# A causal long convolution in a two-block network on one NeuronCore: copies of four shifts in one DMA, four more taps on TensorE for the last chunk, and a layer norm through Ln and Exp

## The reference

```
def conformer_conv(x, pw1_w, pw1_b, dw_w, dw_b, ln_g, ln_b, pw2_w, pw2_b):
    h = x @ pw1_w + pw1_b
    a, g = jnp.split(h, 2, axis=-1)
    h = a * jax.nn.sigmoid(g)
    h = causal_dwconv(h, dw_w, dw_b)      # 31 taps, one filter per channel
    h = layer_norm(h, ln_g, ln_b)
    h = jax.nn.silu(h)
    return h @ pw2_w + pw2_b
```

## Time and profile before

| | us |
|---|---|
| median of 3 runs | 1998.79 (1995.87 to 1998.98) |
| the profiled execution, whole | 1995.84 |
| its span, first to last instruction | 1994.1 |
| pw1 stage, TensorE's slot 0 to the end of taps(7) | 640 to 773 |
| first product of the pw2 stage | 784.04 |

### The profile page before, as it was taken

One profiled execution on the slowest core, in us unless ns is written; L12 is line 12 of the kernel. 1 busy time (PEld: TensorE's weight loads), 2 busy tenths in 40 slices (PEclk: granted clock), 3 DMA queues, 4 the chain that ended last, 5 costly groups with the idle time before them and its releaser, 6 DMA issues.

```text
span 1994.1 us, 23337 instructions
## 1 busy us (share of the span) xinstructions
PE 1902.5 (95%) x9196; PEld 1530.5 (77%) x9196; DVE 1063.6 (53%) x1285; ACT 764.3 (38%) x981; POOL 172.5 (9%) x120
## 2 busy tenths in 40 slices
PE   6999999999999996999999999899899999999996
PEld 4767788877788664888888888788777888888885
DVE  6874442255445788745555533643575545555434
ACT  5532332255324445442223222643673632322223
POOL 5500000000002354010000000200000200000001
PEclk9999999999999998999999999999999999999998
DMA  9211222311222444122322333133002123232321
GB/s 391 85 64 64 84 91 99 105 43 43 85 84 85 129 137 130 64 85 85 105 90 99 105 106 106 64 106 105 2 1 96 64 84 104 85 105 86 125 87 61
DMA packets 32588, 186.38 MB, mean 93 GB/s; under 512 B 4865, under 2 KB 7041, under 8 KB 12034
## 3 DMA queue, kind: packets, MB, share of 16 engines
q1 hardware_dynamic: 30928, 175.90, 26.1%
q10 hardware_dynamic: 1586, 9.44, 1.2%
HBM read 174.64 MB, written 2.10 MB: 89 GB/s over the span
## 4 chain that ended last, share of the span: by engine, by line
PE 87%; ACT 5%; DVE 3%; issue 2%; DMA 1%; POOL 1%; SPq 0%; ACTq 0%; DVEq 0%
PE PS L571 24%; PE PS L573 24%; PE PS L572 24%; PE PS L1064 2%; PE PS L961 2%; PE PS L637 1%; PE PS L638 1%; PE PS L639 1%; DMA RAW<-w 1%; PE PS L931 1%; PE PS L912 1%; ACT X L1474 1%; ACT WH L1110 1%; PE PS L1038 1%; PE PS L1075 1%
## 5 line engine op out<-in xcount | busy, mean ns | idle before, releaser
L571 PE MATMUL PS<-H,WH 128*128 128x512 f32 (+1 forms) x1616 | 625.1, 387 | 26.2 <-POOL L L443 13.2
L572 PE MATMUL PS<-L,WH 128*128 128x512 f32 (+1 forms) x1616 | 617.3, 382 | 0.0
L573 PE MATMUL PS<-H,WL 128*128 128x512 f32 (+1 forms) x1616 | 617.2, 382 | 0.0
L1666 DVE TENSOR_TENSOR WL<-RAW,WH 128x2048 fp32r<-128x2048 f32 x136 | 314.8, 2315 | 269.3 <-ACT WH L1110 265.0
L571 PEld LDWEIGHTS PS<-H,WH 128*128 128x128 f32 x1616 | 305.4, 189 | 98.6 <-issue 18.7
L1110 ACT ACTIVATE WH<-RAW 128x2048 fp32r<-128x2048 f32 x144 | 274.8, 1909 | 238.0 <-PE PS L573 183.4
L573 PEld LDWEIGHTS PS<-H,WL 128*128 128x128 f32 x1616 | 305.2, 189 | 59.2
L572 PEld LDWEIGHTS PS<-L,WH 128*128 128x128 f32 x1616 | 305.4, 189 | 57.2 <-issue 0.8
L443 POOL TENSOR_TENSOR L<-X,H 128x512 fp32r<-128x512 f32 x32 | 46.6, 1463 | 1310.0 <-ACT H L1476 750.8
L1545 ACT ACTIVATE TT<-TT 128x512 f32<-128x512 f32 x44 | 27.8, 632 | 310.3 <-DVE TT L2328 310.3
L571 PE MATMUL PS<-FH,WH 128*128 128x512 f32 (+1 forms) x376 | 142.8, 380 | 0.0
(11 more groups left out here) (339 smaller groups left out, 2483.4 us busy)
## 6 DMA issues: line engine op xcount, KB each, us to landing
RAW<-w SPq DMA_DIRECT2D x148, 1024.0 KB, 4.9
HS<-HC SPq DMA_DIRECT2D x128, 65.5 KB, 2.0
ADA<-w_ada ACTq DMA_DIRECT2D x4, 1024.0 KB, 24.2
ADA<-w_ada SPq DMA_DIRECT2D x4, 1024.0 KB, 23.1
GA<-w_gate SPq DMA_DIRECT2D x1, 4096.0 KB, 18.2
PWR<-w_ple ACTq DMA_DIRECT2D x2, 1024.0 KB, 5.1
out<-X SPq DMA_DIRECT2D x8, 256.0 KB, 2.1
X<-x_t SPq DMA_DIRECT2D x2, 512.0 KB, 6.5
```

The source lines that it names most:

```text
L571: nc.tensor.matmul(ps, wh, xh, start=start, stop=False, skip_group_check=skip)
L572: nc.tensor.matmul(ps, wh, xl, start=False, stop=False, skip_group_check=skip)
L573: return nc.tensor.matmul(ps, wl, xh, start=False, stop=stop, skip_group_check=skip)
L1666: v.tensor_tensor(WL[:, p], RAW[:, p], WH[:, p].bitcast(F32), ALU.subtract).then_inc(w_lo, 1)
```

## The change

Six things are changed.

1. `stack(m)` issues four copies in place of 16. Each has 128 rows by 528 columns and reads each of 32 channel rows four times, at shifts 0 to 3. The diagonal weights are laid out to match.
2. SP's loop has `stack(m)` ahead of `load(pw1+2+m)`.
3. The last chunk has 20 taps on TensorE (20 matmuls, 20 diagonal blocks) and 11 on DVE, whose partial sums for it go to another pair of PSUM banks.
4. ACT squares chunk 5 in `pw1(6)`, behind the diagonals of chunk 7; POOL adds chunks 5 and 6 and their squares ahead of the last `weight_lo`, that of slot pw2+1.
5. TensorE adds the last chunk and its square to the means itself, by products with `CV` and `SQV` behind the product with `ACCV`; the four DVE instructions L2139 and L2143 are gone.
6. The deviation of this norm comes from Ln and Exp on ACT; the two reciprocals on DVE are gone. `I32` is made on POOL, before the w_out stage ends, in place of DVE.

```diff
-HSW = T + TAPS * (QUADS - 1)
+HSW = T + TAPS * QUADS
...
-            for m in range(KC):
+            for m in range(KC - 1):
                 weight_lo(SLOT0["pw1"] + m + 2)
                 if m >= 2:
                     chunk_sum(m - 2)
-                if m >= 2:
                     chunk_squares(m - 2)
-            chunk_sum(KC - 2)
-            chunk_squares(KC - 2)
+            for c in (KC - 3, KC - 2):
+                chunk_sum(c)
+                chunk_squares(c)
+            weight_lo(SLOT0["pw1"] + KC + 1)
...
                 for g in range(4):
-                    for k in range(TAPS):
-                        sp.dma_start(HS[32 * k:32 * k + 32, m % 2, g, :],
-                                     HC[32 * g:32 * g + 32, m, k:k + HSW]).then_inc(hs_in[m % 2], 16)
+                    rows_g = HC[32 * g:32 * g + 32, m, 0:HSW]
+                    shifted = bass.AP(rows_g.tensor, rows_g.offset, [list(rows_g.ap[0]), [1, TAPS], [1, HSW]])
+                    sp.dma_start(HS[:, m % 2, g, :], shifted).then_inc(hs_in[m % 2], 16)
...
             for m in range(KC):
+                stack(m)
                 load(SLOT0["pw1"] + 2 + m)
-                stack(m)
...
-                for q in range(QUADS):
+                quads = QUADS + (m == KC - 1)
+                for q in range(quads):
...
-            ln_stats("conv", 0)
-            ln_stats("conv", 1)
+            pe.wait_ge(cv_sum, KC - 2)
+            pe.wait_ge(cv_sq_sum, KC - 2)
+            for h in range(2):
+                nc.tensor.matmul(PS[:, 4 + h, :], MEANC.to_broadcast([P, P]), ACCV[:, h].rearrange("p a t -> p (a t)"),
+                                 start=True, stop=False, skip_group_check=True)
+            for h in range(2):
+                pe.wait_ge(cv_ready, KC + h)
+                nc.tensor.matmul(PS[:, 4 + h, 0:HT], MEANC.to_broadcast([P, P]), CV[:, KC - 1, cols(h)], start=False,
+                                 stop=True, skip_group_check=True)
+                pe.wait_ge(st_acc, 2 * LN_AFTER["conv"] + h + 1)
+                nc.tensor.matmul(PS[:, 4 + h, HT:T], MEANC.to_broadcast([P, P]), SQV[:, (KC - 1) % 2, cols(h)], start=False,
+                                 stop=True, skip_group_check=True).then_inc(lst_ps, 1)
...
-                if stage == "conv":
-                    a(VAR[:, h], VAR[:, h], ACT.Sqrt, bias=EPS_LN).then_inc(lstd_ready, 1)
-                    return
...
-                if stage == "conv":
-                    own.did(v.reciprocal(PS[:, 4 + h, HT:T], VAR[:, h]))
...
-                taps = DW_K - PE_TAPS
+                tap0 = LAST_TAPS if final else PE_TAPS
+                taps = DW_K - tap0
...
-                    if n == 6 and not (isinstance(s.val(), int) and s.val() == 0):
+                    if n == (4 if final else 6) and not (isinstance(s.val(), int) and s.val() == 0):
...
             ln_var("conv", 1)
+            ln_center(1, 0, CV)
             ln_rstd("conv", 0)
```

More of the change, by code:

```diff
@@ L48 @@
 PE_TAPS = TAPS * QUADS
-HSW = T + TAPS * (QUADS - 1)
+LAST_TAPS = PE_TAPS + TAPS
+HSW = T + TAPS * QUADS
 FFN = 2816
@@ L232, in build @@
         CV = at("CV", A + 20, [P, KC, T])
-        DG = at("DG", A + 36, [P, 2, QUADS, P])
+        DG = at("DG", A + 36, [P, 2, QUADS + 1, P])
         HS = at("HS", A + 44, [P, 2, 4, HSW])
@@ L493, in _ @@
                 nc.gpsimd.tensor_tensor(GA[:, m, :], GA[:, m, :], CROWS[:], ALU.mult).then_inc(gate_mul, 1)
+            nc.gpsimd.memset(I32[:], 1.0).then_inc(i32_ready, 1)
+            for n, (base, cm) in enumerate(((0, 1), (TAPS - 1, -1))):
+                pool.wait_ge(i32_ready, n + 1)
+                nc.gpsimd.affine_select(out=I32[:], in_=I32[:], compare_op=ALU.is_ge, fill=0.0, base=base,
+                                        pattern=[[-TAPS * cm, 32]], channel_multiplier=cm).then_inc(i32_ready, 1)
             ln_lo("w_out", L, X, H)
-            for m in range(KC):
+            for m in range(KC - 1):
                 weight_lo(SLOT0["pw1"] + m + 2)
@@ L661, in ln_stats @@
                     return
-                sums = ACCV if stage == "conv" else ACC
-                nc.tensor.matmul(PS[:, 4 + h, :], MEANC.to_broadcast([P, P]), sums[:, h].rearrange("p a t -> p (a t)"),
+                nc.tensor.matmul(PS[:, 4 + h, :], MEANC.to_broadcast([P, P]), ACC[:, h].rearrange("p a t -> p (a t)"),
                                  start=True, stop=True).then_inc(lst_ps, 1)
@@ L952, in taps @@
                 pe.wait_ge(dg_ready, m + 1)
-                pe.wait_ge(hs_in[m % 2], 16 * 4 * TAPS * (m // 2 + 1))
+                pe.wait_ge(hs_in[m % 2], 16 * TAPS * (m // 2 + 1))
                 if m == KC - 1:
@@ L961, in taps @@
                         mm = nc.tensor.matmul(PS[r, 6 + m // (KC - 1), :], DG[:, p, q, r],
-                                              HS[:, p, g, TAPS * q:TAPS * q + T], start=q == 0, stop=q == QUADS - 1,
+                                              HS[:, p, g, TAPS * q:TAPS * q + T], start=q == 0, stop=q == quads - 1,
                                               skip_group_check=True)
@@ L1413, in diagonals @@
                     act.wait_ge(cp_ps, m - 1)
-                for q in range(QUADS):
+                for q in range(QUADS + (m == KC - 1)):
                     for g in range(4):
@@ L1418, in diagonals, with chunk_square, whole_square @@
                 ins.then_inc(dg_ready, 1)
-            def chunk_square(m, cc=slice(0, T)):
-                a(SQV[:, m % 2, cc], CV[:, m, cc], ACT.Square).then_inc(cv_sq, 1)
+            def chunk_square(m):
+                a(SQV[:, m % 2, :], CV[:, m, :], ACT.Square).then_inc(cv_sq, 1)
+            def whole_square(c):
+                if c < 2:
+                    act.wait_ge(cv_moved, c + 1)
+                else:
+                    act.wait_ge(cv_ready, c + 1)
+                    act.wait_ge(cv_sq_sum, max(c - 2, 1))
+                chunk_square(c)
             def pw1(m):
@@ L1428, in pw1 @@
                 split_hi(Step(0), 1, SLOT0["pw1"] + m + 2)
[L1429 to L1436, removed]
+                if 2 <= m < KC - 1:
+                    whole_square(m - 2)
                 if m + 1 < KC:
                     diagonals(m + 1)
-            act.wait_ge(i32_ready, 1)
+                if m == KC - 2:
+                    whole_square(KC - 3)
+            act.wait_ge(i32_ready, 3)
             diagonals(0)
@@ L1443, in _ @@
                 pw1(m)
[L1444 to L1447, removed]
+            tables("natural_log_exp_and_others")
+            whole_square(KC - 2)
             act.wait_ge(cp_ps, KC)
             load_ple(0)
-            act.wait_ge(cv_sq_sum, KC - 4)
+            act.wait_ge(cv_sq_sum, KC - 3)
             for h in range(2):
                 act.wait_ge(cv_ready, KC + h)
-                chunk_square(KC - 1, cols(h))
+                a(SQV[:, (KC - 1) % 2, cols(h)], CV[:, KC - 1, cols(h)], ACT.Square).then_inc(st_acc, 1)
             def ln_std(stage, h):
@@ L2064, in _ @@
             own.did(v.memset(HC[:, :, 0:PAD], 0.0))
-            v.tensor_tensor(I32[:], SEL[:, 0:32].bitcast(F32), SEL[:, 32:64].bitcast(F32), ALU.add).then_inc(i32_ready, 1)
             def pw1(s):
@@ L2077, in pw1 @@
                 hc = rows(HC, s.val(), 1)
-                dsts = (PS[:, 4:5, :], PS[:, 5:6, :])
-                taps = DW_K - PE_TAPS
+                spare = 2 * (1 - p) if final else 4
+                dsts = (PS[:, spare:spare + 1, :], PS[:, spare + 1:spare + 2, :])
+                tap0 = LAST_TAPS if final else PE_TAPS
+                taps = DW_K - tap0
                 cv = rows(CV, s.val(), 1)
                 for n in range(taps):
-                    k = PE_TAPS + n
+                    k = tap0 + n
                     w_ = dcol("dw_w", s.val(1, k * KC))
@@ L2135, in _ @@
                 v.tensor_tensor(last[:, cols(h)], last[:, cols(h)], PS[:, 7, cols(h)], ALU.add).then_inc(cv_ready, 1)
[L2136 to L2144, removed]
             ln_var("conv", 0)
@@ L2155, in _ @@
                 ln_scale(0, p, CV)
-            for p in range(NP):
+            ln_scale(1, 0, CV)
+            for p in range(1, NP):
                 ln_center(1, p, CV)
@@ L2449, in _params @@
         par[:, PCOL[name]:PCOL[name] + c.shape[1]] = c
-    dw = np.asarray(i["a_dw_w_2"]).reshape(DW_K, KC, 4, 32)[0:PE_TAPS].reshape(QUADS, TAPS, KC, 4, 32)
-    par[:, PCOL["dw_s"]:PCOL["dw_s"] + KC * QUADS * 4] = dw.transpose(1, 4, 2, 0, 3).reshape(P, KC * QUADS * 4)
+    dw = np.asarray(i["a_dw_w_2"]).reshape(DW_K, KC, 4, 32)[0:LAST_TAPS].reshape(QUADS + 1, TAPS, KC, 4, 32)
+    par[:, PCOL["dw_s"]:PCOL["dw_s"] + KC * QUADS * 4] = dw[0:QUADS].transpose(4, 1, 2, 0, 3).reshape(P, KC * QUADS * 4)
+    par[:, PCOL["dw_s"] + KC * QUADS * 4:PCOL["dw_b"]] = dw[QUADS, :, KC - 1].transpose(2, 0, 1).reshape(P, 4)
     par[0:SSM_HEADS, PCOL["small_b"]] = i["dt_bias"]
```

2 lines of the change are left out of this document (1 added, 1 removed).

## The result

| | before | after |
|---|---|---|
| median of the runs | 1998.88 us (4 runs) | 2043.47 us (4 runs, 2042.23 to 2048.18) |
| ratio | | 1.023, interval 1.021 to 1.025 |
| span of the profiled execution | 1994.1 us | 2040.8 us |
| mean granted clock | .989 | .978 |

The changed kernel is 44.6 us slower. The forecast was 2016, with a range up to 2026: the sign and the mechanism held, the size did not.

What follows compares the result with a forecast made beforehand. TensorE bounded the pw1 stage but for three places; the change was to be read on ACT's queue. 8L - 51 with L = 8.8 gave +19.4 on 1995.84, so 2015.2; the forecast was 2016 us, range 2003 to 2026.

Steps and rivals of the forecast that it cites:

- The loop: pw1 stage, through ACT's queue: sigmoid, HC, stack, load, rounding, diagonals, next sigmoid; the last sigmoid comes 22.9 us later.
- L: Time from HC written to load landed: 7.5 us at best, 8.8 taken, 9.5 at most.
- 8L - 51: Change of the whole kernel's time in us: +19.4 with L = 8.8, +9.0 with 7.5, +25.0 with 9.5.
- the 0.4: Norm behind the last chunk: with Ln and Exp on ACT the seventh pair comes 0.4 us earlier.
- The tail: Last sigmoid to ACT's squared mean: 9.4 + L = 18.2 us, 3.1 earlier than the 21.3 before.
- the upper end: L of 9.5 us, for a load queued behind copies whose data move at 233 GB/s; the sum is +25.0.
- The head: stack(0) is out after 2.5 us, not 10.11; taps(0) saves some 4 us, which the late second sigmoid swallows.
- in a shadow: Last chunk: taps(7) with 20 taps ends 14.3 us behind the sigmoid at the latest, the last load's path later.
- Rival 2: pw1 stage: the loads stay covered, L below 6.4 us, and the kernel is faster, 1987 us; chance of faster 0.11.
- some 9 earlier: Part of Rival 2: ACT's squared mean comes some 9 us earlier, stack(7) landing 6.3 instead of 12 after HC.
- Rival 1: Stack copies in pw1: their data hide behind the issues, L = 7.5, so +9.0 and 2005 us; chance 0.2.

Runs made afterwards that it cites:

- after_0213: The changed kernel with its four copies issued in the order of groups 0, 2, 1, 3: 2042.70 us, ratio 1.0212.
- sixty_four: The changed kernel with each copy reading 64 rows twice, so the taps get wrong rows: 2038.85 us, ratio 1.0198.
- wide_source: The changed kernel with each copy reading 128 rows once, so the taps get wrong rows: 2011.06 us, ratio 1.0063.
- swap_only: The kernel before with only the order swapped, each load behind its stack of 16 copies: 2076.54 us, ratio 1.0391.
- load_first: The changed kernel with each load ahead of its stack again, the rest of the change kept: 1991.06 us, ratio 0.9963.
- copies_only: The kernel before with four copies in place of sixteen and `I32` made on POOL, loads still ahead of stacks: 1991.62 us, ratio 0.9967.

## Why the prediction was right in kind and wrong in size

**The loop: right.** Eight loads are waited for, the sigmoids don't wait, the squares of steps 2 and 3 wait for POOL inside the loop (5.85 and 5.84 us, 5.98 forecast), TensorE waits for `WL` (six times, for the three forecast), the gap ahead of taps(7) stays (15.1 us), the square of chunk 6 stands behind the last rounding. The sigmoids stand 18 to 21 us apart, and 25 between steps 2, 3 and 4, for the 15 to 17 and 20 to 23 forecast: wider by about the error in L.

**The formula 8L - 51: right.** L is the mean over the eight steps from the end of the write of `HC` to the start of the rounding; the third column puts it into the formula, the last is the difference of the medians.

| kernel | L, us | 8L - 51 | measured |
|---|---|---|---|
| changed kernel | 11.97 | +44.8 | +44.6 |
| after_0213 | 11.82 | +43.6 | +43.2 |
| sixty_four | 11.37 | +40.0 | +39.3 |
| wide_source | 7.89 | +12.1 | +13.0 |
| swap_only | 15.56 | +73.5 | +78.5 |

Four kernels with the same rest of the stage fall within 1 us of it. swap_only doesn't have the shorter tail for which the 51 stands. Inside the traces, from the first sigmoid to ACT's squared mean, the four take 43.7, 42.5, 38.9 and 11.4 us more than the kernel before. That is 7.9 us for each us of L, and 1.1 to 1.5 us less than the sum has there (8L - 50.6, without the 0.4). So the match with the medians to 1 us has some luck in it, and the factor of eight has not. The tail holds by itself in the changed kernel: 9.4 + 12.0 = 21.4, measured 21.3.

**The step that failed: L.** The prediction took 8.8 and gave 9.5 as the upper end, "1.7 + 4.6 + 3.2", with 4.6 us for the data of four copies "at 233 GB/s" from rows 8. In step 0 of the changed kernel the last of the four copies was issued at 657.77 and landed after 5.4 us, at 663.2: 8.1 us behind the first issue, for 1.7 + 4.6 = 6.3 in the sum. The load landed 3.9 us later, for 3.2:

```profile
L561 SPq DMA_DIRECT2D HS<-HC x1: 1699/1699/1699, 657.8 to 657.8; - x1
...
DMA to landing us min/median/max: 5.4/5.4/5.4
```

So of the 2.5 us beyond the upper end, 1.8 are the copies' data, and 0.7 the load behind them. What failed is first the rate. With the 156 GB/s of the window above, the data would take 6.9 us and the sum give 11.8, near the measured 12.0; that this fits so well is partly luck, as a window of 2 us isn't the whole stack. The same window in after_0213 shows more, with L as long:

```profile
657.00:659.00 2.00, 2.00 (x10) 1.66 (x9) 2.00 (x4) 0.00 (x0) 0.00 (x0) 1.00 0.91 208
```

Rows 8 show copies that read 32 rows once each, with an issue every 0.63 us and engines half idle. I scaled this to full occupation and took the end for an upper bound, with the thought that a full queue would only be kinder. A copy of another shape was rated by a row of the old shape; wide_source shows that the shape alone moves the rate from 156 to more than 300 GB/s. The same item took the issues as 0.63 each: they were 0.67, 0.60, 1.23 and 1.70. That adds nothing to L by itself (after_0213: shorter issues, L of 11.8).

Each us of error in L counts eight times, and the range had only 0.7 us above my value. The bound of the one term that is multiplied by eight should have been the widest. With the row's own rate as it stood (107 GB/s, no scaling) the copies' data would have been 10.1 us, L 15.0 and the far end +69: that was the upper bound that the nearest row gave.

**The head and the tail.** In the changed kernel the formula, which counts nothing for the head, holds. In load_first the head is worth 4.1 us, as forecast. The tail from the last sigmoid is as long as before (21.3 both times), as L ate the "3.1 earlier"; for L = 12 the formula says so itself. Ln and Exp gain 0.5 us at the seventh pair, for the 0.4 forecast. The 20 taps were costed in a shadow and stand in the path once the loop is open: 0.6 to 1.7 us.

**The rivals.** Rival 2, that the loads stay covered, gave 1987; load_first, where they are, is 1991. Of the "some 9 earlier" that it had at ACT's squared mean the head's 4.1 came, but only 2.0 in the tail, as taps(7) starts 8.1 us behind the write of `HC` and not 6.3, and takes 6.91. Rival 1, that the copies' data hide, is wide_source: L = 7.9 and +13 for the forecast 7.5 and +9. The rule of the Trainium skill that stood with rival 1 ("DMA: Bandwidth & Descriptors", "Anatomy of one DMA") is fitted on DMAs issued by GpSimd; these come from SP. It describes the copies with 128 source rows and not those with 32: its 2.0 us plus bytes at 436 GB/s is an estimate of 2.6 us for 270 KB, measured 2.6 in wide_source and 5.0 in the changed kernel. The rule of "Door 1" that stood with the upper end had the direction; by its half rate, an estimate, the copies' data would take 5.0 us, L would be 9.9 and the sum +28, more than the "near +25" of the prediction and less than the measured +44.6.

## What to carry to other kernels

Before a load is moved behind work on its queue, follow who waits for it and whether that engine also feeds the work it was moved behind: if so, the distance is paid once in every turn, and slack that the waits showed before is gone. A transfer that repeats few source rows is not priced by its bytes, nor by a row of another shape; take the rate of the old shape as it stood for the far end, and let the widest range stand at the term with the largest factor. Joining small DMAs is worth having only as far as its landing, not its issue, is what somebody waits for: here it was 6.4 us (copies_only), from two waits for a stack, and one swapped line cost eight times that.

## What the runs showed of the hardware

- A copy inside the memory that writes 128 rows of 2112 bytes lands after 2.6 us when it reads 128 rows once, 4.3 when it reads 64 rows twice, 5.0 when it reads 32 rows four times. These are medians of 32 copies that stand four in a row; the first of the first four landed after 2.3 us with 128 rows and 3.9 with 32.
- In a window of 2 us, such copies on one queue moved 148 GB/s at a share of 0.95 with 32 source rows, and 355 GB/s with 128; with 32 rows in the order 0, 2, 1, 3 it was 208.
- A DMA issue on SP took 0.6 us with none or one of these copies ahead of it, and 1.2 and 1.7 with two and three ahead. The load behind all four then took 0.60 to issue; in the order 0, 2, 1, 3 the four copies took 0.8 us less and the load 1.5 us.
- A load of 1 MiB behind four such copies lands after 7.6 us (median of 8), where the median of all 148 loads is 4.9. Sharing the copies over two queues didn't speed them up: 6.0 us on ACT's, and the wait ahead of the last taps grew from 6.04 to 8.03 us.
